# Weighted values of a bank of turned weights, three banks behind its transposes instead of two

## What is computed

```
# stick-breaking: per head, 128 queries at a time
z = q @ k.T * 64**-0.5
weights = where(mask, exp(log_sigmoid(z) + later), 0);   out = weights @ v
# dilated: softmax over windows (128,1), (512,4), (2048,16), mixed by their denominators
out = softmax(z * scale + log_count) @ v
```

## Time and profile before

| | before |
|---|---|
| median of 3 runs | 2083.41 us |
| profiled execution, its own time | 2083.61 us |
| its span, first to last instruction | 2081.8 us |
| PE busy | 1932.0 us (93%) |
| DVE busy | 1257.5 us (60%) |
| ACT busy | 908.3 us (44%) |
| heads, from the first scores to the last values | 722 to 1298 us of the span |

### The profile page before, as it was taken

How to read it: one execution, slowest core, us unless ns; L and a number is a source line. 1 busy time by engine, 2 the same in 40 slices (tenths; PEclk the granted TensorE clock), 3 DMA queues, 4 the chain that set the end, 5 groups by cost and what they waited for, 6 DMA issues and landing times. The chain is left out here.

```text
span 2081.8 us, 25977 instructions
## 1 busy us (share of the span) xinstructions
PE 1932.0 (93%) x9224; PEld 1582.6 (76%) x9224; DVE 1257.5 (60%) x1649; ACT 908.3 (44%) x1467; POOL 753.1 (36%) x506
## 2 busy tenths in 40 slices
PE   5899999999999898989989976896999999999998
PEld 4788888888888676767767755685788888888886
DVE  6855556555556266676676677327856556554555
ACT  6433333333335455555555555306433333333334
POOL 2656656530000252242242335304656556540000
PEclk9999999999999999999999986897999999999999
DMA  3443544558664310010101112511534435458663
GB/s 143 153 166 131 193 151 144 190 192 290 195 192 144 116 46 26 21 56 25 51 25 40 31 36 70 193 41 71 186 143 160 174 132 185 152 203 308 192 192 142
DMA packets 95584, 276.01 MB, mean 133 GB/s; under 512 B 10480, under 2 KB 14704, under 8 KB 89840
## 3 DMA queue, kind: packets, MB, share of 16 engines
q1 hardware_dynamic: 95472, 274.59, 38.7%
HBM read 190.14 MB, written 80.22 MB: 130 GB/s over the span
## 5 line engine op out<-in xcount | busy, mean ns | idle before, releaser
L703 PE MATMUL banks<-ffn_x_operands_hi 128*128 128x512 f32 x616 | 239.8, 389 | 0.0
L706 PE MATMUL banks<-ffn_x_operands_hi,ffn_x_operands_lo 128*128 128x512 f32 x616 | 239.7, 389 | 0.0
L705 PE MATMUL banks<-ffn_x_operands_lo,ffn_x_operands_hi 128*128 128x512 f32 x616 | 239.6, 389 | 0.0
L1265 DVE TENSOR_TENSOR heads_wt<-banks,heads_wt 128x512 fp32r<-128x512 f32 (+1 forms) x160 | 100.9, 632 | 134.7 <-ACT heads_wt L1109 133.9
L1382 PE MATMUL banks<-first_hi,w_hi 128*128 128x512 f32 x384 | 161.1, 420 | 13.5 <-ACT heads_qk_raw L1131 7.9
L401 ACT ACTIVATE scaled_rows<-banks 128x512 f32<-128x512 f32 x132 | 78.6, 595 | 201.9 <-PE banks L690 201.9
L516 DVE TENSOR_TENSOR scaled_rows<-banks,scaled_rows 128x512 f32<-128x512 f32 x132 | 91.1, 690 | 118.1 <-PE banks L690 74.4
L986 POOL TENSOR_TENSOR scaled_rows<-scaled_rows,heads_stay 128x128 f32<-128x128 f32 (+7 forms) x64 | 86.1, 1351 | 210.9 <-DVE heads_stay L1225 210.9
L1384 PE MATMUL banks<-first_hi,w_lo 128*128 128x512 f32 x384 | 152.2, 396 | 0.0
L1383 PE MATMUL banks<-first_lo,w_hi 128*128 128x512 f32 x384 | 152.0, 396 | 0.0
L687 PE MATMUL banks<-first_hi,ffn_w_ring_hi 128*128 128x512 f32 x352 | 139.1, 395 | 11.8 <-DVE first_lo L567 11.8
(11 more groups left out here) (183 smaller groups left out, 4821.0 us busy)
## 6 DMA issues: line engine op xcount, KB each, us to landing
w_raw<-in_ffn_w_gate SPq DMA_DIRECT2D x22, 1024.0 KB, 6.8
ffn_up_raw<-in_ffn_w_up SPq DMA_DIRECT2D x22, 1024.0 KB, 6.1
ffn_down_raw<-in_ffn_w_down SPq DMA_DIRECT2D x22, 1024.0 KB, 4.9
down_operands<-ffn_down_raw SPq DMA_DIRECT2D x22, 1024.0 KB, 7.3
w_raw<-h_operands SPq DMA_DIRECT2D x52, 256.0 KB, 3.0
ffn_up_raw<-h_operands SPq DMA_DIRECT2D x52, 256.0 KB, 3.0
ffn_down_raw<-h_operands SPq DMA_DIRECT2D x50, 256.0 KB, 3.0
w_raw<-in_w_in SPq DMA_DIRECT2D x24, 512.0 KB, 4.0
```

The costliest lines, as they stand in the source:

```text
L703: pe.matmul(out, hi[:, 0, tok], hi[:, 1, :], start=(opens and c == 0), stop=False, skip_group_check=True)
L705: pe.matmul(out, hi[:, 0, tok], lo[:, 1, :], start=False, stop=False, skip_group_check=True)
L706: last = pe.matmul(out, lo[:, 0, tok], hi[:, 1, :], start=False, stop=(c == NP - 1), skip_group_check=True)
L1265: dve.tensor_tensor(wt[:, wt_slot(s, j), 0:tiles, 1, :], b.ps[:, bank, 0:tiles * P].rearrange("p (t c) -> p t c", c=P), wt[:, wt_slot(s, j ...
```

## The change

The distance is named `BEHIND` and is 3 instead of 2, on PE and in `values_done`, which sets where ACT and DVE evacuate. The first three steps, where no bank three back exists, are taken out of the loop, so its ends move from between steps 1 and 2 to between steps 2 and 3. At the very end three banks of values follow the last transposes. The four slots of `wt` and all other waits stay.

```
+BEHIND = 3
 def values_done(it, kind, s, j):
-    bank = banks_back(it, kind, s, j, 2)
+    bank = banks_back(it, kind, s, j, BEHIND)
     return bank[:3] if bank and bank[3] == banks_of(bank[2]) - 1 else None
...
# on ACT, DVE and PE alike:
-            one_run(0, SB_KIND, 0, 2)
+            one_run(0, SB_KIND, 0, 3)
             with pe.Fori(0, PAIRS - 1) as it:
-                one_run(it, SB_KIND, 2)
+                one_run(it, SB_KIND, 3)
                 one_run(it, DIL_KIND)
-                one_run(it + 1, SB_KIND, 0, 2)
-            one_run(PAIRS - 1, SB_KIND, 2)
+                one_run(it + 1, SB_KIND, 0, 3)
+            one_run(PAIRS - 1, SB_KIND, 3)
...
# in step() on PE:
                     turn_weights(it, kind, s, j, proj)
-                    values_behind(it, kind, s, j, 2)
+                    values_behind(it, kind, s, j, BEHIND)
...
                 if last and s == STEPS - 1:
-                    values_behind(it, kind, s, banks_of(s) - 1, 1)
-                    values_behind(it, kind, s, banks_of(s) - 1, 0)
+                    for n in reversed(range(BEHIND)):
+                        values_behind(it, kind, s, banks_of(s) - 1, n)
```

## The result

The changed kernel takes **2128.36 us** (median of 4 runs, 2125.01 to 2134.8) against 2083.51 us before: a ratio of 1.0219, 95% interval 1.0201 to 1.0237. It is slower by 44.9 us, where 18.1 was forecast, and lies above the forecast's range, which ended at 2113: the direction was right, the size forecast was less than half of the measured one. The profiled execution took 2125.01 us, with a span of 2123.2.

What follows compares the result with a forecast made beforehand. PE is busy 1932.0 of 2081.8 us, so time is PE's work plus its waits, and only waits change. Terms 9.9 + 5.6 + 5.5 - 3.9 + 1 = +18.1 on 2083.61 gave 2101.7 us, range 2090 to 2113.

Steps and rivals of the forecast that it cites:

- a third bank removes no wait: PE's values never wait for their low part in `wt`, so a third bank by itself removes no wait.
- Part 1: Runs 2, 4 and 6: the later store delays the swaps queued behind it and the rotation; +9.9 us (7.8 to 12.3).
- It isn't absorbed: The rotation's delay is not absorbed at step 4's 1.95 us wait, which ends on the same shifted chain.
- The loop ends move for nothing: Moving the loop ends costs nothing, since ACT's fall into its 4.15 us wait ahead of the rotation.
- Part 2: Steps 6 and 7 of four SB runs: additions behind the second scan, a unit missing; +5.6 us (0 to 11.6).
- Part 3: Steps 6 and 7 of DIL runs 1, 3, 5: waits grow without the unit ahead; +5.5 us (4.5 to 6.5).
- Part 4: Gains: waits at 4.2 and step 1's maximum in DIL runs shrink, SB runs put at 0; -3.9 us.
- Part 5: Run 7, which projects nothing: DVE's additions move against normalizations, with gains and losses; +1 us (-3 to +3).
- A: Rival, chance 0.14: the rotation is covered, the queue's cost falls to 1 or 2 us; 2092 to 2094.
- C: Rival, chance 0.07: faster, as the accumulator's waits shrink and the swaps are in time; -11, 2072 us.
- D: Rival, chance 0.05: nothing to see, the other parts' gains and losses cancel and A holds; 2080 to 2088.
- B: Rival, chance 0.13: longer PE waits in steps 3 and 6 also bring half-clock stretches; up to 2112 us.

Runs made afterwards that it cites:

- e3: The changed kernel with SyncE's load of v's weights and four piece-0 swaps ahead of the store that waits for the previous run's last additions; 2121.35 us.
- e5: The changed kernel with e3's queue, loops of PE, ACT and DVE written out, and run 7's store behind the first load of output weights; 2105.5 us.
- e1: The kernel before, distance still 2, with only the loop ends of PE, ACT and DVE moved to between steps 2 and 3; 2093.86 us, ratio 1.0055.
- e2: The changed kernel with ACT's loop alone written out, so that ACT never jumps; 2118.98 us.
- e8: The changed kernel with GpSimd's first-head product in steps 6 and 7 of SB runs made on the last 128 keys alone; 2115.27 us.
- e12: The kernel before with GpSimd's first-head product in steps 6 and 7 of SB runs made on the last 128 keys alone; 2079.81 us, ratio 0.9988.
- e4: The changed kernel with the evacuation of steps 3 to 6 on ACT and DVE one bank earlier, PE's distance still 3; 2121.95 us.
- e9: The changed kernel with the rotation's two DVE operations of steps 4 and 5 behind bank 2 and the additions instead of behind bank 1; 2132.79 us.
- e7: The changed kernel with the single projection units of steps 6 and 7 ahead of bank 3 instead of bank 2; 2121.35 us.
- e6: The kernel before with the loops of PE, ACT and DVE written out, nothing else; 2080.41 us, ratio 0.9985.

## Why the prediction was right in direction and wrong in size

**What bounds the kernel, and that a third bank removes no wait.** Right. The wait for the accumulator grew from 33.6 to 71.5 us; none of the values' matmuls for `wt` had been there to lose.

**Part 1, SP's queue (+9.9).** Right mechanism, near in size. From the end of the additions at 894.16 to the sine's product at 900.93 passed 6.8 us, where the working had 7.6; the addition took 0.69 us once no product ran beside it, where 0.66 was taken. The rule of the Trainium skill (SBUF — State Buffer, Who interferes with whom), that such an addition and a GpSimd operation exclude each other, gave the same choice, and the trace agrees with it. Taking the queue's delay away won 7.0 us (e3). "It isn't absorbed" was wrong in part: steps 2 and 3 paid 12.3 us for the queue, some of which came back later, and the wait of 1.95 us for ACT's copy in step 4 of run 2 is 0.19 after the change. What I missed is that the same store stands ahead of the output weights in run 7. The prediction followed the queue in runs 2, 4 and 6 alone; in run 7 it cost ACT 3.39 us, and mending it is in e5: step 3 of run 7 is 0.8 us longer than before instead of 3.8.

**"The loop ends move for nothing".** Wrong: a term put at 0 that is +10.6 alone (e1), and 9.4 for ACT's in the changed kernel (e2). In the trace of before ACT's next instruction comes 2.7 us after its jump (880.61 to 883.28), but two sigmoids were still queued and covered all but some 0.3 of it. The working took it that ACT would jump while the instruction ahead of the jump still waited for the rotation. It doesn't: in the changed kernel the jump stands in the trace at 902.45, 0.07 us after the waiting instruction started. The same 0.06 or 0.07 us stands in the traces of e1 and e3. Idle time ahead of the waiting instruction didn't cover the jump behind it; the work queued behind the last wait did, in the kernel before. That the price is the jump's own was shown by e1, e2 and by run 6.

**Part 2, steps 6 and 7 of SB runs (+5.6).** Wrong: +18.7 in step 6, while step 7, put at +0.6 a run, came out 1.2 shorter over the four. The failing step is "the scan starts 0.85 us earlier, ends 938.9". It starts earlier and ends when it did, since it meets GpSimd's product, and that scan's end is tied to the product's (2.15 us behind it in both kernels). I had used that very rule on the rotation's addition two paragraphs above, and didn't ask which other DVE operation with two SBUF inputs meets a product. The second failing step is values 5.0: I took about 1 us, "paid back at 5.2". They wait 3.06 us; ahead of the evacuation stands the rotation's addition, 2.15 us with a product beside it. e8 and e12 show the part of the product, 9.7 of the 18.7. e4 shows that the place on ACT and DVE as a whole makes 14.2 of it. That the rest comes from the place behind the rotation is argued from the timeline and not shown: e9, which moved the rotation, won 1.8 there.

**Part 3, DIL runs (+5.5).** The places and waits came as said (0.58 to 1.86, 0.82 to 1.56); in time it was 8.2, 3.9 in step 6 and 4.3 in step 7. But the reason "the unit is missing" holds for step 7 alone: e7 put step 6's unit back and won nothing. There the second exponential stands ahead of the copy on ACT (from 1020.24 for 1.15 us in run 3, the copy at 1021.99, values 6.0 at 1023.51); that it sets the time is read from the timeline and not tested.

**Part 4 (-3.9).** Right for DIL runs: the wait at 4.2 went, that for the maximum fell from 1.50 to 0.69, and steps 0 to 5 of the three runs came out at -4.1. For SB runs, put at 0, steps 4 and 5 came out at -7.4, part of it step 3's delay absorbed; -3.6 stays when that delay is mended (e5).

**Part 5, run 7 (+1; its terms add up to 0.8).** Wrong: +6.8. 3.0 us of it are the queue, by step 3. Steps 6 and 7 are 5.6 us longer where 1.4 and 1.6 were said. DVE's normalizations meet GpSimd's products on the output weights more often there, 4.2 us of DVE's time in four rows; that this is the cause is read from the timeline, and it stays open.

**Rivals.** None of A, C and D came. B, the clock, was no rival but part of the result: PE was busy 10.6 us more, and the stretches at 0.50 grew by 30.7 us, where the prediction named over 10 as a sign of being wrong. It should have stood in the sum, since waits of 3 to 4 us were forecast. Its own sum was off too: three and four times 2.5 us are 17.5, not 11, which gives 2119, still 9 us short. In run 7 the clock was at 0.50 for 41.2 of 68.5 us already before, and for 44.4 of 75.3 after.

## What to carry to other kernels

Moving the place where a buffer is released means following every in-order queue that the release stands in: SyncE's loads behind the store in all runs, the last one too, and the loop's jump on each engine. Work that an engine does while a neighbour blocks it anyway is free; find it before moving it, by comparing ends and not starts (the scan ended 2.15 us behind the product in both kernels). More distance bought nothing here, where the consumer never waited for the producer and the single accumulator stayed single.

## What the runs showed of the hardware

A taken jump on ACT took 2.7 us (before) to 3.8 us (the changed kernel) from the jump to the next instruction (3.30 and 3.45 us of idle "issue" in e1 and the changed kernel), and under 0.1 us when the loop is left. On DVE it took 0.3 us (903.14 to 903.48 in the changed kernel). On PE it is uneven: 0.35 us or so in run 2 of the changed kernel, but 2.81 us of waiting in run 4 and 3.79 in run 2 of e1. With the jumps written out the four runs of e5 lie within 1.3 us, those of the changed kernel within 9.8; but nine of e6's, also written out, lie within 5.8, so that the jumps make the spread isn't shown.
